# A hybrid encoder layer on one core: another order for the stores of the rotated tiles, three low parts, the split of the values and three loads of memory weights

## The chip, the core and the metric

The kernel runs on one core of a Trainium2 chip. It has one instruction stream for each engine: PE (TensorE, matrix products), DVE (VectorE), ACT (ScalarE), POOL (GpSimd) and SP (SyncE), which here issues every DMA. The streams wait for each other by semaphores. The metric is the time of one execution on the device in microseconds (us), the median of several runs.

## The reference

The layer is computed in fp32 for 1024 positions of width 1024. Cut to what matters:

```python
h = rms_norm(x, g_pre)
proj = h @ w_in                      # 1024 x 1024 @ 1024 x 7424, split into
# a_b, a_c, a_x, a_z, b_q, b_k, b_v, b_z, m_q, m_z, gate_logits
ya = short_gated_conv(a_b, a_c, a_x, w_conv) * silu(a_z)
q, k = partial_rope(b_q), partial_rope(b_k)      # rotated: 16 of each head's 64
yb = window_attention_with_sink(q, k, b_v, attn_sink) * silu(b_z)   # +-128 tokens
mk, mv = split(rms_norm(mem, g_mem) @ w_mem_kv, 2)                  # 256 memory tokens
ym = memory_cross_attention(m_q, mk, mv) * silu(m_z)
merged = g0 * (ya @ w_up_a) + g1 * (yb @ w_up_b) + g2 * (ym @ w_up_m)   # g = sigmoid(gate_logits)
return x + rms_norm(merged @ w_out, g_post)
```

## The kernel before

Every large product is made of three PE passes on fp32r operands. A weight block of 128x512 is split into a high part (ACT, `high_part`, L1086, a rounded copy into `ring`) and a low part (POOL, `low_part`, L665, the block minus its high part). The ring has 4 places, so the high part of product n waits until product n - 4 is done. PE waits for high and low part before each product (`product`, L741 to L743: 12 matmuls of 128x128 by 128x512).

The columns of `w_in` are taken as 29 pairs of 128-column tiles. Pairs 0 to 2 (keys, values, four query tiles) are multiplied directly (L753 to L757, blocks A11, A12, A21, A22). From pair 3 on, a Strassen scheme makes each pair from 7 products in the order P1, P2, P6, P7, P4, P5, P3. Numbered over the whole program, the direct products are 0 to 11, pair 3 has 12 to 18, pair 4 has 19 to 25. DVE forms the sums S1, S2, S4 of the weight blocks (L1469 to L1486) and takes each result out of PSUM (`take_c11` L1496, `add_p6` L1501, `add_p7` L1507, `take_c21` L1519, `take_c22`, `take_c12`). Four PSUM places are used in turn, so a product also waits until the one four before it has been taken. SP stores each finished quarter of a pair to DRAM (`store_raw`, L453).

The rotation comes beside pairs 1 to 3. For tile j (0 the keys, 1 to 4 the queries) DVE makes `swap_rows` (L1550), `times_cos` (L1560) and `rotate` (L1564 and L1566), ACT rounds the rotated tile (`rope_high`, L1163), POOL takes the difference (`rope_low`, L686), and SP stores both parts to DRAM in the order that the attention reads (`store_rope`, four DMAs L411 and L413 of 256 KB for a query tile, `rope_stored[j]`). `load_block(0)` (L463, L467, L468) reads the queries and the key windows of the first block of 128 positions back, and needs `rope_stored[0]` to `[3]`. Query tile 4 of that block comes straight from SBUF by `last_queries` (four small DMAs, L478 and L479). The values are turned by PE (`turn_v`, L837) and split by DVE (`make_values`, L1625 and L1628).

The window attention is woven in from pair 4 on, one group of 4 heads and 128 positions for each pair: PE makes the scores ahead of P6 (`scores`, L854 and L855), DVE adds the mask and takes the maximum (`softmax_head`, L1640; for the first group it first waits for `rope_stored[4]`, since the buffer of the probabilities lies over a rotated tile), ACT takes the exponentials (`exps`, L1207 and L1209) and scales them (`normalise`, L1216), and PE turns the probabilities ahead of P3 (`turn_probs`, L862).

After pair 20 come 16 memory steps (`mem_step`, numbered m0 to m15; L906 to L908 are the matmuls of m0 to m7, 128x256 each). Their weights are loaded by `load_m` (L503) into 4 buffers, so the load of step i waits for the low part of step i - 4.

The order of each engine is written out by hand: the engines run the same list `ORDER` of steps (pair, product), and each step has its list of what that engine does in it.

Of the kernel before, what the change touches and what calls it, by code (L numbers as in the profile page):

```python
# [46 lines left out]
P_DIRECT, P_SPILL, P_ATT, P_CONV = 3, 3, 4, PAIRS - 2 * AC  # L47
# [9 lines left out]
M_STEPS = 16  # L57
# [27 lines left out]
NS = len(ORDER)  # L85
# [75 lines left out]
def hybrid_layer(nc, x, mem, w8, wup, wmem, wout, g_pre, g_mem, g_post, w_conv, sink,  # L161
                 cos, sin, mask, ident_in, out):
    ctx = ExitStack()
    with ctx:
# [220 lines left out]
        def _(sp):  # L385
# [167 lines left out]
                sp.dma_start(gate_of(g), raw_d[GATE[g // KC] + g % KC - T_GA]).then_inc(gate_landed[g % 2], 16)  # L553

            for p, name in ORDER[N_DIRECT:]:
                if p == "m":
                    if name + 4 < M_STEPS:
                        load_m(name + 4)
                    if name == M_STEPS - 1:
                        load_mq(0)  # L560
                        load_sm(0)
                    continue
                gr, i = p - P_ATT, p - P_CONV
                if name == "P1":
                    load_spot(A11, p + 1)
                    if p == P_DIRECT:
                        store_rope(3)
                    if p == P_ATT + ATT_GROUPS:
                        for n in range(4):
                            load_m(n)  # L570
                elif name == "P2":
                    load_spot(A12, p + 1)
                    load_spot(A21, p + 1)
                    store_block(p - 1, "next P2")
                    if 1 <= gr <= ATT_GROUPS and gr % 2 == 0:
                        store_attention(gr // 2 - 1)
                    if p > P_CONV:
                        store_cross(i - 1)
                        load_sm(i)
                elif name == "P6":  # L580
                    load_spot(A22, p + 1)
                    store_block(p - 1, "next P6")
                    if p == P_DIRECT:
                        last_queries()
                        load_block(0)
                        store_rope(4)
                    if 0 <= gr < ATT_GROUPS - 1 and gr % 2 == 1:
                        load_block((gr + 1) // 2)
                    if gr == ATT_GROUPS - 1:
                        sp.wait_ge(scored, 4 * ATT_GROUPS)  # L590
                        for b in range(2):
                            sp.dma_start(memx[:, b, :], mem[b * P:(b + 1) * P, :]).then_inc(mem_landed, 16)
                elif name == "P7":
                    store_block(p - 1, "next P7")
                elif name == "P4":
                    if p == P_LAST:
                        load_gate(0)
                elif name == "P5":
                    if 1 <= gr < ATT_GROUPS and gr % 2 == 1:
                        load_sb(gr // 2)  # L600
                    if P_CONV <= p < P_LAST:
                        load_mq(p + 1 - P_CONV)
                store_block(p, name)
# [44 lines left out]
            for b in range(NB - 1):  # L648
                p = b % 2
# [11 lines left out]
        @block.gpsimd  # L661
        def _(pool):
            def low_part(n):
                pool.wait_ge(hi_made, n + 1)
                nc.gpsimd.tensor_tensor(ring[:, n % RING, 1, :], operand(n), ring[:, n % RING, 0, :].bitcast(F32),  # L665
                                        ALU.subtract).then_inc(lo_made, 1)

            def low_of_h(n):
                idx, j, place = H_BLOCKS[n]
                if n < KC:  # L670
                    pool.wait_ge(h_copied, n + 1)
                else:
                    pool.wait_ge(h_copied_act, n - KC + 1)
                pool.wait_ge(h_hi_made, n + 1)
                nc.gpsimd.tensor_tensor(hc[:, idx, 1, j, :], f32(place, HALF), hc[:, idx, 0, j, :].bitcast(F32),
                                        ALU.subtract).then_inc(h_lo_pool, 1)

            def low_of_combination(idx, j):
                nth = SPLITS.index(idx)
                pool.wait_ge(comb_hi, HC * nth + j + 1)  # L680
                nc.gpsimd.tensor_tensor(hc[:, idx, 1, j, :], f32(SUM_AT[idx] + j * HALF, HALF),
                                        hc[:, idx, 0, j, :].bitcast(F32), ALU.subtract).then_inc(comb_pool, 1)

            def rope_low(j):
                pool.wait_ge(rope_hi, j + 1)
                nc.gpsimd.tensor_tensor(rope_low_at[j], rotated(j), rope_high_at[j].bitcast(F32),  # L686
                                        ALU.subtract).then_inc(rope_lo, 1)

            nc.gpsimd.memset(snaps[:, 0, 0:P], 0.0).then_inc(warm_made, 1)
            pool.wait_ge(xs_made, 2)  # L690
            low_part(0)
            low_part(1)
            low_of_h(2)
            low_part(2)
            low_part(3)
            pool.wait_ge(inv_made, 2)
            nc.gpsimd.tensor_scalar(f32(X0 + 5 * D, D), f32(X0 + 5 * D, D), st[:, 9, 5:6], None,
                                    ALU.mult).then_inc(xs_pool, 1)
            for n in POOL_CHUNKS[1:]:
                low_of_h(n)  # L700
            low_part(4)
            low_part(5)
            low_part(6)
            low_part(7)
            rope_low(0)
            low_part(8)
            low_part(9)
            rope_low(1)
            for n in range(10, 14):
                low_part(n)  # L710
            rope_low(2)
            for j in (0, 2):
                low_of_combination(T1, j)
            low_part(14)
            low_part(15)
            rope_low(3)
            low_part(16)
            low_part(17)
            rope_low(4)
            for n in range(18, NS + 3):  # L720
                low_part(n)
            for g in range(UPS):
                if g + 3 < UPS:
                    low_part(NS + g + 3)
                n = y_step(g)
                if n is not None:
                    which, c = divmod(n, AC)
                    pool.wait_ge(y_hi_made, n + 1)
                    nc.gpsimd.tensor_tensor(y_of[1 + which][:, c, 1, :], y_block(n), y_of[1 + which][:, c, 0, :].bitcast(F32),
                                            ALU.subtract).then_inc(y_lo_made, 1)  # L730
# [351 lines left out]
        def _(act):  # L1082
            def high_part(n):
                wait_operand(act, n)
                at_least(act, slot_done, n - RING + 1)
                nc.scalar.activation(ring[:, n % RING, 0, :], operand(n), ACT.Copy).then_inc(hi_made, 1)  # L1086
# [89 lines left out]
            high_part(11)  # L1176
            high_part(12)
            high_part(13)
            rope_high(2)
            high_of_combination(T1)  # L1180
            high_part(14)
            high_part(15)
            wait_slot(act, 2, "A22")
            act.wait_ge(comb_dve, 2 * HC)
            nc.scalar.copy(v_raw, tile_bank(V_TILE)).then_inc(v_copied, 1)
            rope_high(3)

            def block_sigmoid(p, nth, made):
                n = silu_block(p, nth)
# [68 lines left out]
            for n, (p, name) in list(enumerate(ORDER))[N_DIRECT:]:  # L1258
# [12 lines left out]
                    continue  # L1271
                gr, i = p - P_ATT, p - P_CONV
                if name == "P1":
                    if 1 <= gr <= ATT_GROUPS:
                        side(gr - 1)
                    if p - 1 in SILU:
# [4 lines left out]
                        ya_high(0)  # L1281
                        ya_high(1)
                elif name == "P2":
                    if p == P_DIRECT:
                        rope_high(4)
                    if p - 1 in SILU:
                        block_sigmoid(p - 1, 3, c12)
                elif name == "P6":
                    if 0 <= gr < ATT_GROUPS:
                        exps(gr)  # L1290
                    if 0 <= i:
                        cross_exps(i)
                elif name == "P7":
                    if 0 <= gr < ATT_GROUPS:
                        normalise(gr)
                    if p in SILU:
# [78 lines left out]
        def _(dve):  # L1375
# [235 lines left out]
            sum_s4(P_DIRECT)  # L1611
            rotate(3)
            low_of_combination(T1)
            rotate(4)
            dve.wait_ge(small_landed, 64)

# [140 lines left out]
            for p, name in ORDER[N_DIRECT:]:  # L1757
# [22 lines left out]
                    if 1 <= i and i % 2:  # L1780
                        conv_tap(p - 1, 0)
                elif name == "P2":
                    take_c11(p)
                    if 0 <= gr < ATT_GROUPS:
                        softmax_head(gr)
                    if p - 1 in SILU:
# [26 lines left out]
                        conv_tap(p - 1, 1)  # L1813
                elif name == "P4":
                    take_c21(p)
                    if p < P_LAST:
                        sums_first(p + 1)
                        sum_s2(p + 1)
# [19 lines left out]
                elif name == "P3":  # L1838
                    take_c12(p)
                    if p < P_LAST:  # L1840
                        sum_s4(p + 1)
                    if p == P_DIRECT:
                        make_values()
                    if p == P_CONV - 2:
                        scale_mem()
                    if 0 <= i < NB - 1:
                        stage_mq(i + 1)
                    if 0 <= i and i % 2 == 0:
                        conv_product(p)
# [165 lines left out]
```

## Time and profile before

| | |
|---|---|
| median of 3 runs | 942.83 us (941.14 to 943.02) |
| profiled execution | 942.63 us, its span 940.9 us |
| mean granted TensorE clock | 0.996 |
| busy: PE, DVE, ACT, POOL | 98%, 65%, 45%, 41% of the span |
| HBM read, written | 90.46 MB, 33.55 MB |

The span runs from the first to the last instruction of the profiled execution. The trace names each instruction by its line, writes tiles without buffer numbers, and says which engine ended an idle stretch. DMA-issuing instructions stand in the rows of SPq.

### The profile page before, as it was taken

What the parts mean: (1) busy time and instruction counts of PE and PEld (TensorE: products, weight loads), DVE (VectorE), ACT (ScalarE), POOL (GpSimd) and SP (SyncE); (2) the same over time, 40 slices, a digit from 0 to 9 for tenths busy, and PEclk for the clock granted to TensorE, in tenths of its full rate; (3) what the DMA queues carried; (4) which work ended last, traced back from release to release, by engine and by line L of the source; (5) the groups of instructions that cost most, each with busy time, mean ns of one, the idle gap of its engine ahead of it and who ended that gap; (6) DMA issues with size and microseconds to landing.
All of it is one profiled execution on the core that took longest, in us unless ns stands there. A gap on an engine that the chain in (4) does not pass through costs nothing. (4 is left out here: it accounts for less than half of the span.)

```text
span 940.9 us, 12659 instructions
## 1 busy us (share of the span) xinstructions
PE 924.4 (98%) x4440; PEld 777.3 (83%) x4440; DVE 609.6 (65%) x1032; ACT 424.8 (45%) x808; POOL 382.5 (41%) x261
## 2 busy tenths in 40 slices
PE   9999899999999999999999999999999999999997
PEld 8787678888888888888888888888888888888885
DVE  5689776565656566656585178888896368663443
ACT  7623465444444466544462434343443553432211
POOL 3646834444444443444445744444442636200000
PEclk9999999999999999999999999999999999999999
DMA  7243746343525343525253422222222974642222
GB/s 287 90 125 94 195 129 196 101 157 101 165 94 168 102 129 107 195 94 169 99 180 117 143 62 83 83 81 84 80 78 65 337 238 164 204 157 68 90 90 89
DMA packets 81182, 124.45 MB, mean 132 GB/s; under 512 B 7008, under 2 KB 40416, under 8 KB 81120
## 3 DMA queue, kind: packets, MB, share of 16 engines
q1 hardware_dynamic: 81120, 123.65, 40.7%
q8 instruction: 36, 0.59, 0.3%
q14 instruction: 26, 0.21, 0.1%
HBM read 90.46 MB, written 33.55 MB: 132 GB/s over the span
## 5 line engine op out<-in xcount | busy, mean ns | idle before, releaser
L665 POOL TENSOR_TENSOR ring<-spots,ring 128x512 fp32r<-128x512 f32 x218 | 312.7, 1438 | 389.7 <-ACT ring L1086 378.1
L741 PE MATMUL pm<-hc,ring 128*128 128x512 f32 x728 | 286.9, 394 | 1.7 <-POOL ring L665 1.6
L743 PE MATMUL pm<-hc,ring 128*128 128x512 f32 x728 | 284.2, 390 | 0.0
L742 PE MATMUL pm<-hc,ring 128*128 128x512 f32 x728 | 283.6, 390 | 0.0
L1086 ACT ACTIVATE ring<-spots 128x512 fp32r<-128x512 f32 x218 | 135.8, 628 | 247.3 <-PE pm L743 176.1
L741 PEld LDWEIGHTS pm<-hc,ring 128*128 128x128 f32 x728 | 136.8, 188 | 29.4 <-issue 2.9
L743 PEld LDWEIGHTS pm<-hc,ring 128*128 128x128 f32 x728 | 136.7, 188 | 29.0
L742 PEld LDWEIGHTS pm<-hc,ring 128*128 128x128 f32 x728 | 136.9, 188 | 26.8
L1319 ACT ACTIVATE area<-area 128x1024 f32<-128x1024 f32 x24 | 25.4, 1060 | 59.8 <-DMA area<-raw_d 59.8
L1036 PE MATMUL pm<-hc,ring 128*128 128x512 f32 x128 | 49.9, 390 | 0.0
L1037 PE MATMUL pm<-hc,ring 128*128 128x512 f32 x128 | 49.8, 389 | 0.0
L1038 PE MATMUL pm<-hc,ring 128*128 128x512 f32 x128 | 49.8, 389 | 0.0
L1071 PE MATMUL pm<-hc 128*128 128x512 f32 x128 | 49.8, 389 | 0.0
L1072 PE MATMUL pm<-hc 128*128 128x512 f32 x128 | 49.8, 389 | 0.0
L1073 PE MATMUL pm<-hc 128*128 128x512 f32 x128 | 49.8, 389 | 0.0
L1507 DVE TENSOR_TENSOR snaps<-pm,snaps 128x512 f32<-128x512 f32 x26 | 17.9, 690 | 39.4 <-PE pm L743 39.3
L1667 DVE TENSOR_TENSOR area<-pv,area 64x512 f32<-64x512 f32 x16 | 11.0, 689 | 47.8 <-ACT area L1203 47.7
L1209 ACT ACTIVATE area<-area,st 128x384 f32<-128x384 f32 x64 | 38.4, 600 | 0.0
L1859 DVE TENSOR_TENSOR hc<-spots,hc 128x512 fp32r<-128x512 f32 x16 | 25.4, 1585 | 17.6 <-ACT hc L1333 17.5
L1091 ACT COPY snaps<-pm 128x512 f32<-128x512 f32 x26 | 15.2, 585 | 45.7 <-PE pm L743 45.7
L1216 ACT ACTIVATE area<-area,st 128x384 f32<-128x384 f32 x64 | 34.2, 606 | 0.2
L1367 ACT ACTIVATE area<-pm 128x1024 f32<-128x1024 f32 x7 | 7.2, 1029 | 58.0 <-PE pm L1073 58.0
(214 smaller groups left out, 1640.9 us busy)
## 6 DMA issues: line engine op xcount, KB each, us to landing
spots<-in_w SPq DMA_DIRECT2D x116, 256.0 KB, 3.3
raw_d<-area SPq DMA_DIRECT2D x72, 256.0 KB, 2.0
area<-raw_d SPq DMA_DIRECT2D x24, 512.0 KB, 3.7
area<-in_x SPq DMA_DIRECT2D x16, 512.0 KB, 5.2
spots<-in_wup SPq DMA_DIRECT2D x24, 256.0 KB, 3.9
q_d<-area_r SPq DMA_DIRECT2D x16, 256.0 KB, 4.2
area<-raw_d SPq DMA_DIRECT2D x16, 256.0 KB, 3.8
area<-in_wmem SPq DMA_DIRECT2D x16, 256.0 KB, 3.2
```

The source lines that it names most:

```text
L665: nc.gpsimd.tensor_tensor(ring[:, n % RING, 1, :], operand(n), ring[:, n % RING, 0, :].bitcast(F32), ALU.subtract).then_inc(lo_made, 1)
L741: pe.matmul(bank, hi, moving_hi(k), start=(k == 0), stop=False)
L742: pe.matmul(bank, hi, moving_lo(k), start=False, stop=False)
L743: mm = pe.matmul(bank, lo, moving_hi(k), start=False, stop=(k == HC - 1))
L1036: pe.matmul(dst, hi, y[:, at, 0, cols], start=(begin and c == chunks[0]), stop=False)
L1037: pe.matmul(dst, hi, y[:, at, 1, cols], start=False, stop=False)
L1038: mm = pe.matmul(dst, lo, y[:, at, 0, cols], start=False, stop=(end and c == chunks[-1]))
L1071: pe.matmul(dst, hi, wo[:, k, 0, :], start=(k == 0), stop=False)
L1072: pe.matmul(dst, lo, wo[:, k, 0, :], start=False, stop=False)
L1073: mm = pe.matmul(dst, hi, wo[:, k, 1, :], start=False, stop=(k == KC - 1))
L1086: nc.scalar.activation(ring[:, n % RING, 0, :], operand(n), ACT.Copy).then_inc(hi_made, 1)
L1209: ins = nc.scalar.activation(probs[:, h, :], probs[:, h, :], ACT.Exp, bias=st[:, 3, h:h + 1], accum_out=st[:, 5, h:h + 1])
```

## The change

SP, ACT, POOL and DVE do the same work in another order at two places: around pair 3, and at the end of pair 20.

```diff
@@ sync
             for p, name in ORDER[N_DIRECT:]:
+                if p == P_CONV - 1 and name in ("P4", "P5", "P3"):
+                    load_m({"P4": 4, "P5": 5, "P3": 6}[name])
                 if p == "m":
-                    if name + 4 < M_STEPS:
+                    if 7 <= name + 4 < M_STEPS:
                         load_m(name + 4)
...
                 if name == "P1":
                     load_spot(A11, p + 1)
-                    if p == P_DIRECT:
-                        store_rope(3)
...
                     store_block(p - 1, "next P6")
                     if p == P_DIRECT:
+                        store_rope(3)
+                        load_block(0)
                         last_queries()
-                        load_block(0)
                         store_rope(4)
@@ gpsimd
             rope_low(1)
-            for n in range(10, 14):
+            for n in range(10, 15):
                 low_part(n)
             rope_low(2)
             for j in (0, 2):
                 low_of_combination(T1, j)
-            low_part(14)
             low_part(15)
+            low_part(16)
             rope_low(3)
-            low_part(16)
-            low_part(17)
+            for n in range(17, 20):
+                low_part(n)
             rope_low(4)
-            for n in range(18, NS + 3):
+            for n in range(20, NS + 3):
                 low_part(n)
@@ scalar
             high_part(13)
+            high_part(14)
             rope_high(2)
             high_of_combination(T1)
-            high_part(14)
             high_part(15)
             wait_slot(act, 2, "A22")
             act.wait_ge(comb_dve, 2 * HC)
             nc.scalar.copy(v_raw, tile_bank(V_TILE)).then_inc(v_copied, 1)
-            rope_high(3)
...
                 if name == "P1":
+                    if p == P_DIRECT:
+                        rope_high(3)
...
                 elif name == "P2":
-                    if p == P_DIRECT:
-                        rope_high(4)
...
                 elif name == "P7":
+                    if p == P_DIRECT:
+                        rope_high(4)
@@ vector
             rotate(3)
             low_of_combination(T1)
+            take_c11(P_DIRECT)
             rotate(4)
...
                 elif name == "P2":
-                    take_c11(p)
+                    if p > P_DIRECT:
+                        take_c11(p)
...
                 elif name == "P4":
                     take_c21(p)
+                    if p == P_DIRECT:
+                        make_values()
...
                     if p < P_LAST:
                         sum_s4(p + 1)
-                    if p == P_DIRECT:
-                        make_values()
```

On POOL around pairs 2 and 3 (L665 or L666 is a low part, L686 or L687 the low part of a rotated tile, L681 or L682 that of a combination of h) the rows of before are:

```order
L665 TENSOR_TENSOR ring<-spots,ring 128x512 x4
L686 TENSOR_TENSOR area_r<-area,area_r 128x1024
L681 TENSOR_TENSOR hc<-area,hc 128x512 x2
L665 TENSOR_TENSOR ring<-spots,ring 128x512 x2
L686 TENSOR_TENSOR area_r<-area,area_r 128x1024
L665 TENSOR_TENSOR ring<-spots,ring 128x512 x2
L686 TENSOR_TENSOR area_r<-area,area_r 128x1024
```

and now:

```order
L666 TENSOR_TENSOR ring<-spots,ring 128x512 x5
L687 TENSOR_TENSOR area_r<-area,area_r 128x1024
L682 TENSOR_TENSOR hc<-area,hc 128x512 x2
L666 TENSOR_TENSOR ring<-spots,ring 128x512 x2
L687 TENSOR_TENSOR area_r<-area,area_r 128x1024
L666 TENSOR_TENSOR ring<-spots,ring 128x512 x3
L687 TENSOR_TENSOR area_r<-area,area_r 128x1024
```

Low part 14 moved ahead of the third rotated tile, and low parts 16, 18 and 19 each moved ahead of a later one.

On SP around pair 3 (`spots` are weight blocks, L411 and L413 are `store_rope`, L478 and L479 `last_queries`, L463 to L468 `load_block(0)`) the rows of before are:

```order
L398 DMA spots<-in_w 128x512 [waits s_made,lo_made]
L411 DMA q_d<-area_r 64x8x128 [waits rope_lo]
...
L413 DMA q_d<-area_r 64x8x128
L398 DMA spots<-in_w 128x512 [waits s_made,lo_made] x3
L478 DMA area_r<-area_r 64x128 [waits rope_lo,rope_stored2]
...
L479 DMA area_r<-area_r 64x128
L463 DMA area_r<-q_d 128x2x384 [waits rope_stored3,rope_stored2,zero_stored,rope_stored1,rope_stored0]
L467 DMA area_r<-kh_d 128x2x384
L468 DMA area_r<-kl_d 128x2x384
L411 DMA q_d<-area_r 64x8x128 [waits rope_lo]
```

and now:

```order
L398 DMA spots<-in_w 128x512 [waits s_made,lo_made] x4
L411 DMA q_d<-area_r 64x8x128 [waits rope_lo]
...
L413 DMA q_d<-area_r 64x8x128
L463 DMA area_r<-q_d 128x2x384 [waits rope_stored3,rope_stored2,zero_stored,rope_stored1,rope_stored0]
L467 DMA area_r<-kh_d 128x2x384
L468 DMA area_r<-kl_d 128x2x384
L478 DMA area_r<-area_r 64x128 [waits rope_lo,rope_stored2]
...
L479 DMA area_r<-area_r 64x128
L411 DMA q_d<-area_r 64x8x128 [waits rope_lo]
```

Three weight loads moved ahead of the fourth rotated tile's store, and `load_block(0)` ahead of `last_queries`.

On SP at the end of pair 20 (L453 stores a finished quarter, L503 is `load_m`) the rows of before are:

```order
L398 DMA spots<-in_w 128x512 [waits s_made,lo_made]
L453 DMA raw_d<-area 128x512 [waits c21]
L453 DMA raw_d<-area 128x512 [waits c22]
L453 DMA raw_d<-area 128x512 [waits c12]
L503 DMA area<-in_wmem 128x512 [waits lo_made] x12
```

and now:

```order
L398 DMA spots<-in_w 128x512 [waits s_made,lo_made]
L503 DMA area<-in_wmem 128x512 [waits lo_made]
L453 DMA raw_d<-area 128x512 [waits c21]
L503 DMA area<-in_wmem 128x512 [waits lo_made]
L453 DMA raw_d<-area 128x512 [waits c22]
L503 DMA area<-in_wmem 128x512 [waits lo_made]
L453 DMA raw_d<-area 128x512 [waits c12]
L503 DMA area<-in_wmem 128x512 [waits lo_made] x9
```

The loads of m4, m5 and m6 moved ahead of one store each.

## Rows read from the trace of the kernel before

**Rows 1.** The page, part 1: busy us, share of the span, instructions.
```profile
PE 924.4 (98%) x4440; PEld 777.3 (83%) x4440; DVE 609.6 (65%) x1032; ACT 424.8 (45%) x808; POOL 382.5 (41%) x261
```

**Rows 2.** Waits of PE: line, releaser, total us, times, longest us.
```profile
PE sa L854 <- DVE area_r L1628: 3.4, 1, 3.4
PE sa L906 <- POOL ring L665: 1.8, 1, 1.8
```

**Rows 3.** Busy time by stretch: length, engines' busy us, granted clock, DMA share, GB/s.
```profile
100.00:120.00 20.00, 16.24 (x71) 12.70 (x70) 14.49 (x24) 8.75 (x14) 15.15 (x10) 1.00 0.87 238
119.00:123.00 4.00, 3.82 (x19) 3.42 (x20) 3.69 (x19) 0.63 (x1) 0.00 (x0) 1.00 0.91 291
```

**Rows 4.** Timeline of PE: start us, us, instruction, idle before and releaser.
```profile
94.67 0.47 PE L741 MATMUL pm<-hc,ring 128*128 128x512 f32 x1 [1.39 <-POOL ring L665]
...
119.18 0.41 PE L854 MATMUL sa<-area_r 128*128 128x384 f32 x1 [3.41 <-DVE area_r L1628]
...
131.57 1.48 PE L862 MATMUL sa<-ident,area 128*128 128x128 f32 x12
```

**Rows 5.** Timeline of POOL beside the rotation.
```profile
85.97 2.41 POOL L686 TENSOR_TENSOR area_r<-area,area_r 128x1024 fp32r<-128x1024 f32 x1 [5.93 <-ACT area_r L1163]
88.34 3.98 POOL L681 TENSOR_TENSOR hc<-area,hc 128x512 fp32r<-128x512 f32 x2
92.28 3.95 POOL L665 TENSOR_TENSOR ring<-spots,ring 128x512 fp32r<-128x512 f32 x2
...
103.52 2.42 POOL L686 TENSOR_TENSOR area_r<-area,area_r 128x1024 fp32r<-128x1024 f32 x1
```

**Rows 6.** Timeline of DVE, pairs 2 to 4.
```profile
83.57 1.23 DVE L1566 TENSOR_TENSOR area<-area 128x1024 f32<-128x1024 f32 x1
...
91.20 2.20 DVE L1566 TENSOR_TENSOR area<-area 128x1024 f32<-128x1024 f32 x1
...
102.27 0.68 DVE L1496 TENSOR_TENSOR area<-pm,snaps 128x512 f32<-128x512 f32 x1
...
116.05 0.74 DVE L1625 CAST area_r<-sa 128x256 fp32r<-128x256 f32 x2
...
119.84 0.69 DVE L1496 TENSOR_TENSOR area<-pm,snaps 128x512 f32<-128x512 f32 x1 [0.20 <-DMA raw_d<-area]
120.45 0.55 DVE L1640 CUSTOM_DVE_ANT_0 area<-sa,maskb 128x384 f32<-128x384 f32 x1
...
122.91 0.16 DVE L1648 TENSOR_TENSOR st<-sinkb,st 128x4 f32<-128x4 f32 x1
```

**Rows 7.** Timeline of ACT, the first group's softmax.
```profile
123.67 0.63 ACT L1086 ACTIVATE ring<-spots 128x512 fp32r<-128x512 f32 x1 [3.31 <-PE pm L743]
...
128.66 2.14 ACT L1216 ACTIVATE area<-area,st 128x384 f32<-128x384 f32 x4
```

**Rows 8.** Timeline of SP's queue, pairs 3 and 4; then the landing of its last row.
```profile
101.33 1.23 SPq L413 DMA_DIRECT2D q_d<-area_r  x1
...
113.65 1.17 SPq L413 DMA_DIRECT2D q_d<-area_r  x1
...
DMA to landing us min/median/max: 5.4/5.4/5.4
```

**Rows 9.** Memory steps by stretch (columns as in rows 3), and PE's timeline.
```profile
505.00:508.00 3.00, 3.00 (x27) 3.00 (x26) 2.21 (x4) 0.38 (x1) 1.29 (x1) 1.00 0.41 153
513.40:516.90 3.50, 3.50 (x18) 3.36 (x18) 0.84 (x2) 1.90 (x4) 3.50 (x4) 0.51 0.50 150
...
512.55 0.35 PE L906 MATMUL sa<-area_r,ring 128*128 128x256 f32 x1 [1.76 <-POOL ring L665]
```

**Rows 10.** Timelines of SP, ACT and POOL ahead of step m4.
```profile
507.04 15.56 SPq L503 DMA_DIRECT2D area<-in_wmem  x12
...
510.44 0.63 ACT L1086 ACTIVATE ring<-area 128x512 fp32r<-128x512 f32 x1 [5.06 <-DMA area<-in_wmem]
...
511.15 1.26 POOL L665 TENSOR_TENSOR ring<-area,ring 128x512 fp32r<-128x512 f32 x1 [4.39 <-ACT ring L1086]
```

## The prediction, made before the changed kernel was run

> **What bounds the kernel now.** I read the page's part on busy time first: PE is busy for 924.4 of 940.9 us [rows 1], so a change of order can win only what PE idles, 16.5 us, and what its clock loses. Then the waits of PE: two of the longest are the one ahead of the first scores (3.4 us, released by the split of the values) and one in the memory steps (1.8 us, released by a low part) [rows 2]. PE's timeline adds a wait of 1.39 us ahead of product 14 (P6 of pair 3), released by its low part [rows 4]. The table by stretch shows for 100 to 120 us 3.76 us without PE work, 0.35 more than the 3.41 at the scores, spread over starts that low parts hold up [rows 3, 4]. So the head's order costs 1.39 + 3.41 + 0.35 = 5.15 us. The memory steps cost 1.76 us, and then the clock is granted at 0.51 for 3.5 us: that is the 1.2 GHz level, against 2.4 before [rows 9]. In that stretch 18 matmuls ran, where 27 took 3.0 us at full clock, so 31.5 would have: 13.5 matmuls of 0.111 us, 1.5 us lost.
>
> **Part by part.** Nothing is added or removed; four streams are reordered.
>
> *Low part 14 earlier, with its high part.* Its place in the ring comes free about 82 us (product 10, one step of 5.4 us before the first Strassen product), and POOL stands idle for 5.93 us before 85.97 [rows 5], so it is ready by 85.5 instead of 94.3. The wait of 1.39 goes. What is late next is low part 15: POOL takes it after the two combinations, at 92.3, where 14 stood [rows 5], done at 92.28 + 3.95 / 2 = 94.3; PE wants it at 94.67 - 1.39 and the 2.8 us of product 14 and more than half a microsecond of the turning of the values later, at 96.6. Low parts 16 to 19 then come ahead of each need by a microsecond or so, since 16 and 18 no longer stand behind a rotated tile of 2.4 us. That takes the 0.35 as well.
>
> The cost of it: low part 14 now runs beside the third rotation. Such an operation of DVE takes 1.23 us alone and 2.20 beside POOL's work [rows 6], so the rotation chain may come 0.97 later, less what POOL no longer does beside the fourth. The Trainium skill says why ("SBUF — State Buffer", section on who interferes with whom): a VectorE operation with both inputs in SBUF and a GpSimd read take the same port as an exclusive lock, held for the whole instruction. By that rule the loser waits for one whole low part, about 1.3 us, and the sum below would be 0.3 worse than with the row's 0.97; the trace agrees in kind, not to the tenth.
>
> *take_c11 of pair 3 ahead of the last rotation.* It came at 102.27, after that rotation [rows 6]. P5 needs the place it frees at about 102.1 in the faster flow, so without this edit the gain would stop there. It puts 0.7 us ahead of the last rotation. That rotation then ends at about 103 to 104 instead of 102.3, and its low part on POOL, 105.94 before [rows 5], at about 107.5 to 108, since low parts 18 and 19 now stand before it.
>
> *make_values after take_c21.* It runs from 116.05 for 3.0 us, behind the sums of pair 4, which wait for weight blocks that landed late because they were issued behind the fourth rotated tile's store. Now it starts at about 105 and the loads come before that store. The values are ready at about 108, and PE reaches the scores at 119.18 - 5.15 = 114.0. So the 3.41 goes at this place. Next there are the key windows: SP waits for the fourth tile's store to land, last issue 101.33 plus at most the 5.4 us of a later one, 106.7 [rows 8]; the block's three DMAs and the four small ones follow, and the last lands at 113 to 114. This costs 0 to 1 us, and what follows hides it.
>
> *Where the head's gain stops.* softmax_head of the first group waits until the last rotated tile is stored, and before it the store of the first quarter of pair 3 must land (0.20 us waited at 119.84) [rows 6]; that is queued behind the rotated tile's four DMAs, whose last went out at 113.65 and landed 5.4 us later, at 119.05 [rows 8]. From the end of rope_low at 105.94 [rows 5] SP needed 7.7 us for the eleven DMAs up to that one. Now the same eleven begin when the fourth tile has landed, 106.7: the last goes out at 114.4, 0.7 later than before. So the softmax starts at 120.45 + 0.7 = 121.15, not earlier, though PE is 5 us ahead. It takes 122.91 + 0.16 - 120.45 = 2.62 on DVE. ACT lost 1.2 us there before, because the exponentials stood behind a high part that waited for PE until 123.67 and ended at 124.30 [rows 7]; with PE ahead this goes. From 124.30 to 128.66 (table, exponentials, sums) are 4.36 us, and scaling takes 2.14 [rows 7]. So the probabilities are ready at 121.15 + 2.62 + 4.36 + 2.14 = 130.3. PE would come to turn them at 131.57 - 5.15 = 126.4 and waits there 3.9 us. Before, it came at 131.57 without a wait [rows 4]. The head's gain is therefore 131.57 - 130.3 = 1.3 us, not 5.15. Bounds: with SP not late and the stores landing 1 us sooner, as the three weight loads (768 KB) are gone from their side, 2.9; with both the lock's microsecond and a landing 0.3 later, 0. I take 1.3, nearest to the rows as they stand.
>
> After that the chain of each group starts from PE's scores, as before, and nothing stands on an absolute time until the memory steps.
>
> *Three memory loads between the stores.* The load of m4 went out at 507.04, behind three stores that wait for pair 20's results, and ACT and then PE waited for it (high part at 510.44, low part at 511.15, matmul at 512.55) [rows 9, 10]. Now m4's load waits only for the low part of m0, made four products ahead of PE, and lands well before 507. What is late next is the ring: m3 ends at 512.55 - 1.76 = 510.8, a step of 12 matmuls takes 12 x 0.111 = 1.3, so m0 is done at about 506.8; high part 0.63 and low part 1.26 [rows 10] make m4 ready at 508.7, where PE wants it at 510.8. m5 and m6 likewise, each issued ahead of a store and a step or more before its ring place is free; m7's load goes out where m4's did, lands at 510.4, waits for m3's ring place until 510.8, is ready at about 512.7 and wanted at 510.8 + 3 x 1.3 = 514.7. So the 1.76 goes, and with it, I take it, the fall of the clock that came right behind it, 1.5 (bounds 0 and 1.5: no row shows these steps without a wait). No store waits longer: each load's own wait is over before the result that the store waits for.
>
> Sum against the profiled execution of 942.63 (span 940.9 and 1.7 around it): 942.63 - 1.3 - 1.76 - 1.5 = 938.1. The median of the runs, 942.83, is 0.2 above that execution, well inside their spread.
>
> **The rivals.** *The clock falls in the new wait, or falls in the memory steps all the same.* PE stands 3.9 us ahead of the turning of the probabilities. For it: 1.76 us were enough at the memory steps. Against it: the clock stayed at 1.00 right after the 3.41 us at the scores [rows 3], the wait nearest in length and place, so I count nothing. Price 1.5: 939.6.
>
> *The head keeps its whole 5.15.* That needs the last rotated tile in DRAM by about 116; against it speaks SP's row of DMAs. Time 942.63 - 5.15 - 3.26 = 934.2.
>
> *The memory loads do nothing*, because POOL and the ring hold m4 to m7 as late as the loads did. POOL's low part takes 1.26 of a step's 1.33 us. Only the head's 1.3 is left: 941.3.
>
> *Slower: SP stands before load_block(0).* Everything behind it (the last queries, the last rotated tile, pair 3's stores, pair 4's next weights) now waits for the fourth tile's landing, which used to be over when SP came. Each microsecond that it lands after 106.7 moves the first softmax by one. To make the kernel slower by over 1.9 us it must eat 1.3 + 3.3 + 1.9 = 6.5, so land after 113.2. The four DMAs would need 12 us where 5.4 was seen; the time would be 944.6 or more.
>
> **How the numbers follow.** Forecast 0.55, clock 0.25, whole head 0.07, memory steps without gain 0.08, slower 0.05. The forecast's own range is 936.4 (head 2.9) to 939.4 (head 0). The range reaches to 935.8 below, and to 940.8 above for the clock's case with a poor head; outside stay the whole head and most of the two last. A measurement tells about 0.2% from no change, 1.9 us, so faster means under 940.9: 0.55 + 0.25 + 0.07 + 0.02 = 0.89; same 0.07; slower 0.04.
>
> **What would show it.** Right: no wait ahead of product 14; the scores within 1 us of 114; softmax_head released by a DMA near 120 to 121; a wait of PE on ACT's scaling at L862 (new line number 863) of 3 to 4 us; no wait of PE in the memory steps and clock 1.00 there. Wrong: turn_probs reached without a wait (the head's gain is then larger), a scores wait of several microseconds on a DMA, or m4 still released late by POOL.

## The result and the profile after

| | before | after |
|---|---|---|
| median | 942.75 us (941.14 to 943.45, 6 runs) | 936.23 us (935.99 to 937.37, 6 runs) |
| ratio, 95% interval | | 0.9934 (0.9921 to 0.9947) |
| profiled execution, span | 942.63, 940.9 us | 937.37, 935.6 us |

The change makes the kernel 6.5 us faster. The forecast was 4.5 us (938.1): the result lies in the stated range of 935.8 to 940.8, and 0.2 below the forecast's own range, which ended at 936.4. A second profile of the changed kernel, taken with the last experiments, has a span of 934.6. The busy time of PE is nearly the same as in [rows 1]:

```profile
PE 922.4 (99%) x4440; PEld 775.7 (83%) x4440; DVE 612.7 (65%) x1032; ACT 425.5 (45%) x808; POOL 380.9 (41%) x261
```

The waits of PE in the first profile after; they answer to [rows 2]:

```profile
PE sa L863 <- ACT area L1216: 1.7, 1, 1.7
...
PE sa L855 <- DMA area_r<-area_r: 1.0, 1, 1.0
```

The waits for a low part are gone, ahead of P6 as ahead of m4. What stands there now is a wait at the turning of the probabilities, for ACT's scaling, and a smaller one at the first scores, for the last queries. PE's timeline, as in [rows 4]:

```profile
114.91 0.44 PE L855 MATMUL sa<-area_r 128*128 128x384 f32 x1 [0.96 <-DMA area_r<-area_r]
...
129.21 1.53 PE L863 MATMUL sa<-ident,area 128*128 128x128 f32 x12 [1.70 <-ACT area L1216]
```

PE reached the scores 4.3 us earlier than before and the turning only 2.4 earlier. In this execution its first product of w_in began 0.6 later than before (15.6 against 15.0); in the second profile it began at 14.9, and the turning 2.67 earlier than at 131.57:

```profile
128.90 1.53 PE L863 MATMUL sa<-ident,area 128*128 128x128 f32 x12 [1.70 <-ACT area L1216]
```

In between, in the first profile, SP, DVE and ACT (as [rows 8], [rows 6] and [rows 7]):

```profile
114.41 1.27 SPq L413 DMA_DIRECT2D q_d<-area_r  x1
...
DMA to landing us min/median/max: 5.3/5.3/5.3
```

```profile
120.70 0.69 DVE L1498 TENSOR_TENSOR area<-pm,snaps 128x512 f32<-128x512 f32 x1 [3.54 <-DMA raw_d<-area]
121.32 0.55 DVE L1643 CUSTOM_DVE_ANT_0 area<-sa,maskb 128x384 f32<-128x384 f32 x1
...
123.77 0.16 DVE L1651 TENSOR_TENSOR st<-sinkb,st 128x4 f32<-128x4 f32 x1
```

```profile
120.10 1.28 ACT L1207 ACT_TABLE_LOAD   x1
123.96 0.21 ACT L1207 ACTIVATE st<-st 128x4 f32<-128x4 f32 x1 [2.58 <-DVE st L1651]
...
127.02 2.13 ACT L1216 ACTIVATE area<-area,st 128x384 f32<-128x384 f32 x4
```

The last store of the rotated tile goes out at 114.41 (forecast 114.4) and lands at 119.7, DVE stands 3.54 us at take_c11 for the store queued behind it, and the softmax starts at 121.32 (forecast 121.15). New against the forecast is ACT's first row: the table of the exponential is loaded at 120.10, while ACT waits for DVE, and no longer in the chain. In the kernel before it stood in the chain, right behind the high part that ended at 124.30:

```profile
124.32 1.28 ACT L1207 ACT_TABLE_LOAD   x1
125.61 0.20 ACT L1207 ACTIVATE st<-st 128x4 f32<-128x4 f32 x1
```

The memory steps, as [rows 9, 10], first by stretch, then SP's queue:

```profile
502.50:505.50 3.00, 3.00 (x25) 3.00 (x26) 2.37 (x4) 1.17 (x2) 1.85 (x2) 1.00 0.48 157
513.40:516.90 3.50, 3.50 (x20) 3.01 (x20) 0.42 (x1) 1.64 (x4) 3.42 (x4) 1.00 0.66 215
```

```profile
495.79 0.33 SPq L503 DMA_DIRECT2D area<-in_wmem  x1
497.63 0.33 SPq L453 DMA_DIRECT2D raw_d<-area  x1
499.37 0.33 SPq L503 DMA_DIRECT2D area<-in_wmem  x1
502.95 0.33 SPq L453 DMA_DIRECT2D raw_d<-area  x1
503.32 0.43 SPq L503 DMA_DIRECT2D area<-in_wmem  x1
504.33 0.33 SPq L453 DMA_DIRECT2D raw_d<-area  x1
```

Each load now stands ahead of a store, and the clock is 1.00 throughout. On ACT the high parts of m4 and m5 start when their ring place is free (released by PE, L909). Those of m6 and m7 wait for their loads:

```profile
505.67 0.63 ACT L1087 ACTIVATE ring<-area 128x512 fp32r<-128x512 f32 x1 [0.81 <-PE sa L909]
...
507.18 0.63 ACT L1087 ACTIVATE ring<-area 128x512 fp32r<-128x512 f32 x1 [0.60 <-DMA area<-in_wmem]
509.25 0.63 ACT L1087 ACTIVATE ring<-area 128x512 fp32r<-128x512 f32 x1 [1.44 <-DMA area<-in_wmem]
```

PE does not wait for either. The steps up to the first product with the value weights (L918, now L919) ran from 504.8 to 520.0 before and from 502.5 to 514.1 after: 3.6 us less. With the 2.67 of the head this makes the 6.3 by which the second profile's span is shorter.

### The profile page after: what moved, and what is told of

Its sections match the earlier page's. It is cut to its first block, busy times and chain, and to the rows that moved or that the text cites. A ratio compares the mean times of both kernels' runs of the same rounds, so it can differ in the third digit from the quotient of the medians.

```text
span 935.6 us, 12658 instructions
## 1 busy us (share of the span) xinstructions
PE 922.4 (99%) x4440; PEld 775.7 (83%) x4440; DVE 612.7 (65%) x1032; ACT 425.5 (45%) x808; POOL 380.9 (41%) x261
## 4 chain that ended last, share of the span: by engine, by line
PE 87%; DVE 3%; DMA 3%; POOL 2%; ACT 2%; SPq 1%; issue 1%; DVEq 0%; ACTq 0%
PE pm L744 16%; PE pm L742 16%; PE pm L743 16%; PE pm L1074 3%; PE pm L1038 3%; PE pm L1037 3%; PE pm L1072 3%; PE pm L1039 3%; PE pm L1073 3%; PE sa L863 2%; PE pv L875 2%; PE sa L1038 2%; PE sa L1037 2%; PE sa L1039 2%; PE pv L954 2%; PE sa L934 1%
## 5 line engine op out<-in xcount | busy, mean ns | idle before, releaser
L666 POOL TENSOR_TENSOR ring<-spots,ring 128x512 fp32r<-128x512 f32 x218 | 313.0, 1439 | 393.7 <-ACT ring L1087 381.9
L1863 DVE TENSOR_TENSOR hc<-spots,hc 128x512 fp32r<-128x512 f32 x16 | 22.3, 1396 | 21.9 <-ACT hc L1335 21.9
```

## The experiments

The kernels were timed in three groups, each on its own chip and in turns with the kernel before (medians there 943.80, 943.35 and 943.62). So ratios are compared between groups, microseconds within one. The changed kernel has two ratios, 0.9934 from the result and 0.9924 from the third group; between groups, a difference smaller than theirs (0.9 us) is not shown.

**Each half alone.** The head alone: the changed kernel with this undone:

```diff
-                if p == P_CONV - 1 and name in ("P4", "P5", "P3"):
-                    load_m({"P4": 4, "P5": 5, "P3": 6}[name])
-                    if 7 <= name + 4 < M_STEPS:
+                    if name + 4 < M_STEPS:
```

> The changed kernel with its memory loads put back (m4 to m6 again after pair 20's stores). My theory, two separate gains: the head gives 2.4 to 3.0 us and the memory steps 3.3 to 3.6, so this one runs at 942.75 - 2.7 = 940.0 (939.3 to 940.6), with PE's wait of about 1.8 us ahead of m4 back and the clock falling behind it. Rival, the head's gain is given back later and all of the 6.5 us came from the memory steps: 942.75, no faster than before.

Measured: 940.30 us, ratio 0.9963 (0.9949 to 0.9977). The rival is out. By stretch, the memory steps and the turning:

```profile
513.40:516.90 3.50, 3.50 (x31) 3.50 (x31) 0.45 (x2) 1.64 (x4) 3.50 (x4) 1.00 0.60 173
129.50:133.00 3.50, 3.29 (x14) 3.19 (x15) 2.66 (x6) 3.47 (x6) 0.80 (x1) 0.54 0.00 0
```

```profile
PE sa L905 <- POOL ring L664: 2.3, 1, 2.3
PE sa L861 <- ACT area L1214: 2.3, 1, 2.3
```

Both waits were 2.3 us. The clock fell behind the one at the turning, not behind the one ahead of m4: there my expectation missed.

The memory loads alone: the kernel before with the same three lines put in.

> The kernel before with only the three memory loads moved. My theory: 942.75 - 3.5 = 939.2 (938.7 to 939.9), no wait ahead of m4, clock at full in the memory steps, and waits of PE at P6 of pair 3 and at the first scores as before (1.4 and 3.4 us). Rival, the clock falls there whatever PE waits: only the wait of 1.8 us goes, 941.0.

Measured: 940.43, ratio 0.9965 (0.9951 to 0.9979). The wait ahead of m4 is gone and the steps ran at clock 1.00. The time is 1.2 above my expectation, on a chip whose kernel before was 1.05 slower; the ratio is 3.3 us, near the 3.5 expected. In this profile the clock fell at the 3.3 us of waiting ahead of the scores instead, and stayed at half for 6.8 us:

```profile
118.00:124.00 6.00, 5.15 (x14) 4.69 (x15) 4.67 (x20) 0.63 (x1) 0.15 (x1) 0.50 0.73 244
```

The halves add up: 3.5 and 3.3 against 6.2 to 7.2 for both (0.9934 and, in the third group, 0.9924).

**One edit of the head undone.** take_c11 of pair 3 back in step P2:

```diff
             low_of_combination(T1)
-            take_c11(P_DIRECT)
             rotate(4)
```

> The changed kernel with take_c11 of pair 3 back behind the last rotation. My theory, the head ends in one chain (fourth tile's landing, SP's eleven DMAs, last landing, first softmax, turning) and PE waits 1.7 us at its end, so a new wait of PE ahead of it is absorbed: PE waits about 1.5 us at P5 of pair 3 and 0 to 0.3 at the turning, time as the changed kernel's, within 0.3. Rival, each wait counts by itself: 1.5 us slower than the changed kernel.

Measured: 938.62, ratio 0.9938 (0.9925 to 0.9950).

```profile
PE sa L863 <- ACT area L1216: 2.6, 1, 2.6
PE pm L742 <- DVE area L1498: 1.5, 1, 1.5
```

PE waited the 1.5 at P5 as expected, and the time shows little of it: 0.4 us by the ratio against the changed kernel's 0.9934, 1.3 against its 0.9924. That does not part the theories by itself. The wait at the turning did not shrink: pair 3's first quarter landed 6.0 us after its store was issued, where it took 4.9 in the changed kernel, so the softmax started at 122.06, and the clock fell at that wait. Inconclusive in the time; in the trace the new wait at P5 took the place of the one at the first scores (none there any more), and not of the one at the turning. The executions fall in two sets, which the median hides: three at 938.62 to 938.86 with a mean granted clock of 0.996 or 0.997, and 936.58 and 937.30 with 0.998 and 0.999.

make_values back behind take_c12 and the sums:

```diff
                 elif name == "P4":
                     take_c21(p)
-                    if p == P_DIRECT:
-                        make_values()
...
                         sum_s4(p + 1)
+                    if p == P_DIRECT:
+                        make_values()
```

> The changed kernel with make_values back behind take_c12 and the sums. My theory: the values are ready at about 115.5, near the 114.9 at which the key windows and last queries let the scores start anyway, so the scores move by 0.5 to 1 and the turning not at all: time as the changed kernel's, within 0.4. Rival, the early values brought the 3.4 us of that wait: 1.5 us slower or more.

Measured: 939.60, ratio 0.9951 (0.9938 to 0.9965): 1.6 us slower than 0.9934 (2.5 against 0.9924), the rival's figure. My expectation missed.

```profile
PE sa L855 <- DVE area_r L1631: 4.2, 1, 4.2
```

The values were ready at 117.6, 2 us later than I reckoned: on DVE the first three sums of pair 4 stood ahead of them, beside POOL's work, and took 5.3 us (0.85, 2.77 and 1.77, where the changed kernel had 1.57, 0.69 and 0.69). PE came to the turning at 132.5 without a wait, part of it because the clock had fallen at 116.1, within the 4.2 us of waiting.

SP's order around pair 3 as before:

```diff
+                    if p == P_DIRECT:
+                        store_rope(3)
...
-                        store_rope(3)
-                        load_block(0)
                         last_queries()
+                        load_block(0)
                         store_rope(4)
```

> The changed kernel with SP's old order around pair 3 (fourth tile's store ahead of the three weight loads, last queries ahead of load_block). My theory: the block's loads now stand behind the wait for the last low part (108.5) and go out at 111 to 113, so the key windows land at about 118.5 and the scores start 3.5 us later than the changed kernel's, the last tile's store lands 1.5 to 2 us later; time 1.7 to 2.5 us over the changed kernel's. Rival, SP's order costs nothing: as the changed kernel's.

Measured: 940.31, ratio 0.9960 (0.9947 to 0.9972): 2.5 us slower than 0.9934, at the upper end of what was expected, and 3.4 slower than 0.9924, beyond it.

```profile
PE sa L856 <- DMA area_r<-kl_d: 4.0, 1, 4.0
```

```profile
112.03 0.61 SPq L468 DMA_DIRECT2D area_r<-kl_d  x1
...
115.39 1.64 SPq L413 DMA_DIRECT2D q_d<-area_r  x1
```

The key window's load goes out at 112.03, behind the last queries' wait, and PE waits 4.0 us for it.

**One edit alone.** The kernel before with high and low part 14 ahead of the third rotated tile:

```diff
-            for n in range(10, 14):
+            for n in range(10, 15):
                 low_part(n)
...
-            low_part(14)
             low_part(15)
```

> The kernel before with only high part 14 and low part 14 ahead of the third rotated tile. My theory: the wait of 1.4 us ahead of P6 goes and the one at the first scores grows by as much, and by up to 1 us more because the rotation beside the low part takes 1 us longer: no faster than before, 0 to 1.0 us slower. Rival, the wait counts by itself: 1.4 us faster than before.

Measured: 942.88, ratio 0.9999 (0.9991 to 1.0008). No gain:

```profile
PE sa L853 <- DVE area_r L1627: 2.4, 1, 2.4
PE pm L740 <- POOL ring L665: 1.6, 2, 1.3
PE pm L740 <- DVE area L1495: 0.8, 1, 0.8
```

The time came as expected, the way to it did not. I had put the wait of P6 at the first scores, which would have grown; they started at 118.91 (119.18 before), and the wait there fell from 3.41 to 2.40. Ahead of P4, P5 and P3 there are now 0.4, 0.8 and 1.3 us of waiting, 2.5 together, where P6 and P3 had 1.6. The further microsecond that I allowed for did not show in the time.

**What ends the head.** DVE takes the first maximum ahead of take_c11 of pair 4:

```diff
                 elif name == "P2":
+                    if gr == 0:
+                        softmax_head(gr)
                     if p > P_DIRECT:
                         take_c11(p)
-                    if 0 <= gr < ATT_GROUPS:
+                    if 0 < gr < ATT_GROUPS:
                         softmax_head(gr)
```

> The changed kernel with DVE taking the first group's maximum (softmax_head) ahead of take_c11 of pair 4. My theory: in the changed kernel DVE stood at take_c11 until pair 3's first quarter was stored (120.6 us), while the last rotated tile was in DRAM at 119.7; now the softmax starts at 119.8 instead of 121.3, and PE's wait of 1.7 us at the turning of the probabilities falls to 0.1 to 0.3: 936.2 - 1.5 = 934.7. Rival, that wait is set by ACT (table, exponentials, scaling behind its other work): the softmax starts earlier and PE waits as before, 936.2.

Measured: 934.86 (934.51 to 935.51), ratio 0.9909 (0.9896 to 0.9923).

```profile
118.81 0.55 DVE L1643 CUSTOM_DVE_ANT_0 area<-sa,maskb 128x384 f32<-128x384 f32 x1 [2.57 <-issue]
```

```profile
126.97 1.53 PE L863 MATMUL sa<-ident,area 128*128 128x128 f32 x12
```

The softmax starts 2.5 us earlier than in the first profile after, and PE turns the probabilities at 126.97 without a wait.

The last rotated tile's store taken away (in its place the sine table is copied early):

```diff
+            for g in range(2):
+                for own in (slice(0, HEAD), slice(HEAD, P)):
+                    sp.dma_start(q_d[:, own, g, 3, :].rearrange("b p q -> p b q"),
+                                 sin[own, :].rearrange("p (b q) -> p b q", b=NB)).then_inc(rope_stored[4], 16)
...
                         last_queries()
-                        store_rope(4)
```

> The changed kernel without the store of the last rotated tile at its place; the sine table is copied there early, so the fourth query of each head group is wrong from the second block on (left out: that store, 1 MB). It takes the landing away that the first softmax waits for. My theory: softmax_head starts with the scores or when pair 3's first quarter has landed (about 117), PE does not wait at the turning of the probabilities: 936.2 - 1.7 = 934.5 or a little less, if the key windows land sooner too. Rival, the wait has another cause than this store (ACT): 936.2.

Measured: 935.16, ratio 0.9918 (0.9902 to 0.9933).

```profile
116.62 0.68 DVE L1501 TENSOR_TENSOR area<-pm,snaps 128x512 f32<-128x512 f32 x1
117.23 0.55 DVE L1646 CUSTOM_DVE_ANT_0 area<-sa,maskb 128x384 f32<-128x384 f32 x1
```

```profile
126.46 1.47 PE L866 MATMUL sa<-ident,area 128*128 128x128 f32 x12
```

Neither landing holds DVE now, and PE does not wait at the turning. So that store, with the one queued behind it, set the end of the head; ACT did not.

**The first link of that chain.** Four kernels in one group: the changed kernel, the softmax ahead of take_c11, POOL's low part of the fourth rotated tile ahead of low part 16, and both.

```diff
             low_part(15)
-            low_part(16)
             rope_low(3)
-            for n in range(17, 20):
+            for n in range(16, 20):
                 low_part(n)
```

> The changed kernel again, to have it on the same chip as the next three and to see its clock in a second profile. My theory: 0.993 of the kernel before. As the granted clock fell in other runs right behind whichever wait of PE was longer than about 1.7 us, it may or may not fall behind the wait of 1.7 us at the turning; if it does, that execution is 1.5 us longer.

> The kernel with softmax_head ahead of take_c11 of pair 4 again, on the same chip as the changed kernel. My theory: 1.5 us faster than the changed kernel and more steady, since PE has no wait over 1.3 us between the start and the output. Rival: the difference seen before was that of two chips, 0.

> The changed kernel with POOL making the low part of the fourth rotated tile ahead of low part 16. My theory, the chain that ends the head begins with that tile's landing: it lands about 1.7 us earlier, SP's eleven DMAs and the first softmax with it, PE waits 0.6 us more at P4 of pair 3 for low part 16, and the wait at the turning goes from 1.7 to about 0: 1.0 to 1.7 us faster than the changed kernel. Rival, the last rotated tile (its low part at 108.5) sets the chain: the same time, or 0.6 slower for the new wait.

> Both: softmax_head ahead of take_c11, and the low part of the fourth rotated tile ahead of low part 16. My theory: with the first the turning no longer waits, so of the second only the wait of 1.3 us at the first scores is left to win, against 0.6 us new at P4: 0 to 0.7 us faster than with the first alone. Rival, the two add up: 1.5 us faster than with the first alone.

| | median (range) us | ratio, 95% interval |
|---|---|---|
| changed kernel | 936.40 (936.06 to 937.00) | 0.9924 (0.9910 to 0.9939) |
| softmax ahead of take_c11 | 935.37 (935.30 to 935.53) | 0.9912 (0.9896 to 0.9929) |
| low part of the fourth tile first | 936.93 (936.64 to 938.02) | 0.9930 (0.9913 to 0.9947) |
| both | 935.73 (935.55 to 936.04) | 0.9916 (0.9900 to 0.9933) |

The first pair differs by 1.0 us (1.5 was expected) with ranges apart: the softmax first is the best version found, and the cause is not the chip. The third kernel missed its expectation: it is 0.5 us slower than the changed kernel, with ranges that overlap, and not 1.0 to 1.7 faster. So did the fourth: 0.4 slower than the second, where 0 to 0.7 faster was expected. SP's queue of the third, then of the changed kernel:

```profile
93.94 5.95 SPq L398 DMA_DIRECT2D spots<-in_w  x3
99.94 0.59 SPq L411 DMA_DIRECT2D q_d<-area_r  x1
```

```profile
94.09 3.25 SPq L398 DMA_DIRECT2D spots<-in_w  x3
99.82 0.59 SPq L411 DMA_DIRECT2D q_d<-area_r  x1
```

The tile's low part was ready 1.9 us earlier, but the last weight load, which stands ahead of the store on SP since the change, waits for low part 16, and that had been moved back. The store went out at 99.94, no earlier, and PE waited 0.4 more at P4. So this run tested another thing than I meant, and that its time is the rival's says nothing for the rival. That the chain starts at the fourth tile's landing rests on SP's rows (load_block at 107.44, right behind the landing of 102.73 + 4.6) and was not shown by moving it. The rival, that the last tile's low part sets the chain, has the trace of the changed kernel against it: that low part was done at 106.11 + 2.41 = 108.5, and SP came to the DMAs that need it only at 109.41, right behind the block's three.

## Why the prediction was right, and where a size was off

*What bounds it.* Right: the gain was what PE idled and lost in clock at two places, and the halves alone give 3.5 and 3.3 us.

*Low part 14, take_c11, make_values, SP's order.* No wait ahead of P6, as said. The scores started at 114.91, said was 114.0 and up to 1 us of wait for the last landings. The price of low part 14 beside the rotation was in the rows: the third rotation's second operation took 2.27 us (1.23 before), which is 1.04, near the row's 0.97. It is below the 1.3 us that the prediction worked out by the rule in the Trainium skill ("SBUF — State Buffer", "Who interferes with whom"). Low part 14 alone gained nothing (0.9999), as a wait in front of a later, longer one should, though the waits that replaced it stood at three products and not at the scores.

*Where the head's gain stops.* Right in the mechanism: the last store's time, 114.4, and the softmax's, 121.15 against 121.32, came as worked out, and taking the store away removed the wait at the turning. That they agree so closely is partly luck: SP came to load_block at 107.44, not at 106.7, and needed 7.0 us and not 7.7 from there to the last store; in the second profile it was 106.81 and 7.2. The mis-sized term is the 4.36 us from the maximum's end to the scaling, read from before with the table load of 1.28 in it. It measured 127.02 - 123.93 = 3.09: with PE ahead, ACT loads the table while it waits for DVE. I had counted ACT's high part as freed, not the load behind it. The probabilities were ready 1.2 us before the forecast 130.3, and the head gained 2.4 (first profile) and 2.7 (second), not 1.3. The sign that was to show the forecast right, a wait of 3 to 4 us at the turning, missed for the same reason: the wait was 1.7, because the probabilities were ready 1.2 earlier and PE, which had waited 0.96 at the scores, came at 127.5 and not at 126.4.

*The memory loads.* Right in what PE sees: it waits for none of m4 to m7, and 3.6 us are gone against 3.26 forecast. Two steps on the way were off. m6's load was not there before its ring place: it went out at 503.32, landed 3.8 us later, and ACT stood idle 0.60 us until it and 1.44 until m7's, both with time to spare for PE. And the clock's part was sized from a count that takes in matmuls cut by the edges of the stretch (27 in 3.0 us, so 0.111 us each); in the kernel before these matmuls start 0.12 us apart at full clock:

```profile
505.12 0.28 PE L908 MATMUL sa<-area_r,ring 128*128 128x256 f32 x1
505.24 0.28 PE L906 MATMUL sa<-area_r,ring 128*128 128x256 f32 x1
```

A stretch of 3.4 us at half the clock then costs 1.7 us and not 1.5; with the wait of 1.76 that is 3.5 of the 3.6. Both parts went in the profiles, but the clock's part is not tied to this place, see below.

*Rivals.* The whole head was not kept: 2.7 of 5.15. The clock stayed up in both profiles after. SP's wait ahead of load_block stayed short: the fourth tile landed at 107.3, 0.6 later than reckoned (106.7 in the second profile). Sum with the true sizes: 2.67 + 3.6 = 6.3, measured 6.5 between the medians.

## What to carry to other kernels

When a chain of one wait is removed, walk on to the next thing that has an absolute end (here a store's landing), and compare PE's new arrival with it; a single edit ahead of it may be worth nothing (low part 14), and the edits do not add up: undoing three of them one at a time cost 0.4 to 1.3, 1.6 to 2.5 and 2.5 to 3.4 us, more together than the 3.5 of the whole head. In reading a stretch's price from a trace, take out what only stood in it because the engine came late, a table load too. On a queue that waits in order, a load moved ahead of a store ties the store to whatever the load waits for.

## What the runs showed of the hardware

The clock's fall behind a wait of PE is not tied to one place, nor to a length of wait that parts the cases. From 90 us on, eleven of the profiles (before, two of the changed kernel, eight of the experiments) hold fourteen waits of PE of 1.7 us or more. The granted clock fell from 2.4 to 1.2 GHz behind seven of them (1.8, 2.3, 2.4, 2.6, 3.3, 4.0 and 4.2 us) and stayed at 2.4 behind the other seven (1.7, 1.7, 1.8, 2.3, 2.4, 2.6 and 3.4). It stood at half for 3.4 us at the four shorter of the first seven, and for 6.8 at the three longest. In four cases (2.6, 3.3, 4.0 and 4.2) it fell before the wait was over, so PE ran at half for less than that: 3.0 us in the first of them and 5.2 to 6.0 in the others. So a wait of this size costs, beside itself, a fall in some executions and none in others; what decides it these runs don't tell.

The mean granted clock, recorded for every execution, shows the falls where there is no profile. The profiles with no such fall have a mean of 0.998 or 0.999, those with one of 3.4 us 0.996 or 0.997, those with one of 6.8 us 0.995. All eleven executions of the changed kernel are at 0.998 or 0.999. Of the 36 of the kernel before in the three groups, 33 are at 0.996 or less, and 17 of them at 0.993 or 0.994, so with more at half clock than the one fall in its profile. A part of the gain is therefore falls that no longer happen, and not at the memory steps alone; how large a part is not shown.

The spread of the times comes partly from there. The kernel without the last tile's store had no wait at the turning in its profile, yet times from 933.92 to 937.71: its four executions at 0.998 took 933.92 to 935.25, and the two at 0.997 and 0.996 took 937.29 and 937.71. The kernel with the softmax first, timed in two groups, waited little (one profile no longer than 1.3 us, the other 1.8 with the clock at full), stayed at 0.998 or 0.999, and its times spread least in each group (934.51 to 935.51, and 935.30 to 935.53). It is not the whole: the kernel with the fourth tile's low part first took 936.64 to 938.02, all at 0.998 or 0.999.
